# Seven-product turns with two weight buffers: another order of VectorE and ScalarE around cast and low part, the first down slab loaded in halves, the down unit begun on six tiles

## The reference, cut to what matters

```python
def swiglu(h, w_gate, w_up, w_down):
    return (jax.nn.silu(h @ w_gate) * (h @ w_up)) @ w_down
...
h = modulate(rms_norm(x, norm_ffn1[i]), sh1, sc1)
x = x + 0.5 * gt1[:, None, :] * swiglu(h, ffn1_gate[i], ffn1_up[i], ffn1_down[i])
...
h = modulate(rms_norm(x, norm_ffn2[i]), sh3, sc3)
x = x + 0.5 * gt3[:, None, :] * swiglu(h, ffn2_gate[i], ffn2_up[i], ffn2_down[i])
```

## Time and profile before

| | |
|---|---|
| median of 3 runs | 1463.26 us (1463.21 to 1464.64) |
| profiled execution, its own time | 1461.96 us |
| its span, first to last instruction | 1460.4 us |
| TensorE busy | 1380.3 us, 95% |
| VectorE busy | 1011.8 us, 69% |
| ScalarE busy | 571.6 us, 39% |
| mean granted clock of TensorE | 0.985 of full speed |

### The profile page before, as it was taken

The page is one execution under the profiler, slowest core; times in us unless marked ns, Lnnn a source line. Parts: engine busy times, 40 slices in busy tenths (PEclk is TensorE's granted clock), DMA queues, the critical chain, the costliest instruction groups (busy, mean ns, idle before and its releaser), DMA issues. The chain is left out here.

```text
span 1460.4 us, 28232 instructions
## 1 busy us (share of the span) xinstructions
PE 1380.3 (95%) x11590; PEld 1327.8 (91%) x11590; DVE 1011.8 (69%) x1619; ACT 571.6 (39%) x813; POOL 80.1 (5%) x120
## 2 busy tenths in 40 slices
PE   6999998999899999999999999999999999899986
PEld 5899997998898999999899997999899999899986
DVE  5447777358646588998998997855645877457745
ACT  5423454235435322534243337332532345225433
POOL 6100000000001000000000000000000000000000
PEclk9999999999999999999999999999999999999998
DMA  9754664462374222223334444526222231322221
GB/s 320 236 175 148 197 202 148 130 212 90 96 222 139 88 86 78 90 70 102 122 125 146 149 153 160 187 87 202 87 72 80 92 120 59 116 86 88 77 97 59
DMA packets 133210, 189.45 MB, mean 130 GB/s; under 512 B 5133, under 2 KB 113057, under 8 KB 132898
## 3 DMA queue, kind: packets, MB, share of 16 engines
q1 hardware_dynamic: 111900, 112.55, 24.5%
q0 software_dynamic: 17136, 66.87, 13.7%
q10 hardware_dynamic: 4070, 8.57, 1.6%
HBM read 173.73 MB, written 15.18 MB: 129 GB/s over the span
## 5 line engine op out<-in xcount | busy, mean ns | idle before, releaser
L1714 DVE TENSOR_TENSOR w_lo<-raw,w_hi 128x1024 fp32r<-128x1024 f32 x152 | 186.0, 1224 | 262.9 <-ACT w_hi L1244 262.9
L1244 ACT CAST w_hi<-raw 128x1024 fp32r<-128x1024 f32 x152 | 158.9, 1046 | 409.7 <-PE pu L652 380.3
L652 PE MATMUL pu<-h_hi,w_hi 128*128 128x260 f32 x1408 | 287.7, 285 | 4.6 <-DVE work L2443 2.8
L652 PE MATMUL pu<-h_hi,w_lo 128*128 128x260 f32 x1408 | 283.5, 283 | 0.0
L652 PE MATMUL pu<-h_lo,w_hi 128*128 128x260 f32 x1408 | 282.8, 282 | 0.0
L652 PEld LDWEIGHTS pu<-h_hi,w_hi 128*128 128x128 f32 x1408 | 216.9, 188 | 8.7 <-DVE w_lo L1714 4.9
L652 PEld LDWEIGHTS pu<-h_hi,w_lo 128*128 128x128 f32 x1408 | 216.8, 188 | 0.0
L652 PEld LDWEIGHTS pu<-h_lo,w_hi 128*128 128x128 f32 x1408 | 216.6, 188 | 0.0
L652 PE MATMUL pu<-f_hi,w_hi 128*128 128x260 f32 x704 | 146.3, 290 | 22.7 <-DVE f_lo L2020 22.7
L2168 DVE SCALAR_TENSOR_TENSOR d<-u,cw,d 128x512 f32<-128x512 f32 x240 | 163.1, 745 | 0.1
L652 PE MATMUL pu<-f_hi,w_lo 128*128 128x260 f32 x704 | 144.2, 287 | 0.0
(11 more groups left out here) (356 smaller groups left out, 2564.7 us busy)
## 6 DMA issues: line engine op xcount, KB each, us to landing
raw_a<-in_w_ada POOLq DMA_DIRECT2D x30, 1024.0 KB, 7.8
raw<-in_w_in SPq DMA_DIRECT2D x28, 1024.0 KB, 5.2
raw<-in_ffn_gate SPq DMA_DIRECT2D x32, 512.0 KB, 4.0
raw<-in_ffn_up SPq DMA_DIRECT2D x32, 512.0 KB, 5.0
raw<-in_ffn_down SPq DMA_DIRECT2D x16, 1024.0 KB, 5.4
gates_d<-sg_lb ACTq DMA_DIRECT2D x24, 260.0 KB, 2.5
raw<-in_ffn_up SPq DMA_DIRECT2D x6, 1024.0 KB, 5.4
raw<-in_ffn_down SPq DMA_DIRECT2D x8, 768.0 KB, 4.3
```

The costliest lines, as they stand in the source:

```text
L652: last = mm(pu[p][:, e, 0:HALF], w[p][:, k, :], m[:, k, e * HALF:(e + 1) * HALF], start=(at_k == 0 and j == 0), stop=(at_k == k_tiles - 1 ...
L1244: nc.scalar.copy(w_hi[p][:], raw[:, slot, :, p * P:(p + 1) * P]).then_inc(s_hi, 1)
L1714: V.tensor_tensor(w_lo[p][:], raw[:, slot, :, p * P:(p + 1) * P], w_hi[p][:].bitcast(F32), ALU.subtract).then_inc(s_lo, 1)
```

## The change

Seven edits in one:

1. On ScalarE the cast of hidden row 0 (L1372) moves from P1's place to P2's, behind the cast of the next block; the copies of adaLN rows go behind it. In the last turn Silu of row 0 goes ahead of the cast of the second down block.
2. On VectorE L2077 moves from behind the low part at P3 to ahead of it; L2066 from behind the low part at P2 to ahead of that at P5; L2049 from ahead of the low part at P4 to behind it; the low part of hidden row 1 (L2020) from P7's place to P2's, ahead of the low part, and that of row 0 behind it.
3. The weight sums of P3 and of P5 move from ahead of a low part to behind it, at the same position.
4. The sum of P3 uses the slot of that of P5 (`SUM_OF`), with a wait for the block that was there before (`BEFORE_IN_SLOT`).
5. In the last turn L2020 of row 1 and L2026 go ahead of the low part of the second down block.
6. SyncE loads the first down slab in two halves: the upper four row tiles when the last turn's sum of P6 is formed, the lower four when its P4 block is split. The first turn's loads go slot by slot.
7. The first down unit behind the turns begins when six of its tiles are there.

```diff
-SUM_OF = {P5: 0, P6: 1, P7: 2, P3: 3}
+SUM_OF = {P5: 0, P6: 1, P7: 2, P3: 0}
+BEFORE_IN_SLOT = {P5: P3, P6: P6, P7: P7}
@@ SyncE, loads
+                        if it == 0:
+                            for slot, w in enumerate((wg, wu)):
                                 sp.wait_ge(s_lo, n0 - 2 + 2 * slot)
+                                half_of(it, 0, s_raw0, slot, w)
+                                half_of(it, 1, s_raw1, slot, w)
+                            continue
+                        sp.wait_ge(s_wsum, 4 * (t - 1) + SUM_COUNT[P6])
                         rows_of(it, 0, s_raw0)
+                        sp.wait_ge(s_blo, TURN * (t - 1) + P4 + 1)
                         rows_of(it, 1, s_raw1)
+                    sp.wait_ge(s_wsum, 4 * t + SUM_COUNT[P6])
+                    sp.dma_start(raw[:, 0, 0:4, :], cols(wd, 0, 4, r0)).then_inc(s_raw0, 16)
                     sp.wait_ge(s_blo, TURN * t + P4 + 1)
-                    load(Lin(n0), 0, cols(wd, 0, r0=r0))
+                    sp.dma_start(raw[:, 0, 4:KT, :], cols(wd, 0, 4, r0 + 4 * P)).then_inc(s_raw[0], 16)
                     load(Lin(n0 + 2), 1, cols(wd, 256, r0=r0))
@@ TensorE, down unit
-                                 ready=(s_a, a0, GROUPS[g] - 1) if c == 0 else None, swap=g > 0 and c == 0)
+                                 ready=(s_a, a0, GROUPS[g] - (2 if g else 1)) if c == 0 else None, swap=g > 0 and c == 0)
@@ ScalarE, gate_turns
+                def silu_row0(t):
+
+                    act.wait_ge(s_c12, t + 1)
+                    af(gate[:, 0, :], gate[:, 0, :], ACT.Silu).then_inc(s_sg, 1)
...
-                        else:
-                            k = pos - P4
-                            split_hi(Lin(at[f"down{which}_{g}"] + k), k, 0)
+                        elif pos == P4:
+                            split_hi(Lin(at[f"down{which}_{g}"]), 0, 0)
                         if pos == P1:
                             nc.scalar.copy(halves(sg[:, 0, :]), psum(0)).then_inc(s_p1, 1)
-                            if it:
-                                hidden_hi(t - 1, it - 1, 0, 3)
-                        if pos == P2:
-                            ada_part(0, ADA_UP[g] + 2 * it, None)
+                        if pos == P2 and it:
+                            hidden_hi(t - 1, it - 1, 0, 3)
...
                             hidden_hi(t, it, 1, 2)
-                            act.wait_ge(s_c12, t + 1)
-                            af(gate[:, 0, :], gate[:, 0, :], ACT.Silu).then_inc(s_sg, 1)
+                            silu_row0(t)
                             if last:
+                                split_hi(Lin(at[f"down{which}_{g}"] + 1), 1, 0)
                                 hidden_hi(t, it, 0, 3)
+                        if pos == P2:
+                            ada_part(0, ADA_UP[g] + 2 * it, None)
@@ VectorE, add_weights
+                j = TURN * t + P5 if pos == P3 else TURN * (t - 1) + BEFORE_IN_SLOT[pos]
...
-                if t:
-                    dve.wait_ge(s_blo, TURN * (t - 1) + pos + 1)
+                if j >= 0:
+                    dve.wait_ge(s_blo, j + 1)
@@ VectorE, gate_turns: ahead of the low part
+                        if pos == P3 and last:
+                            right_half_row0(t)
+                            hidden_lo(t, it, 1, 2 * it + 1)
+                            multiplied_row0(t)
+                        if pos == P3 and not last:
+                            right_half_row0(t)
                         if pos == P2 and it:
-                            hidden_lo(t - 1, it - 1, 0, 2 * it)
+                            hidden_lo(t - 1, it - 1, 1, 2 * it - 1)
                         if pos == P5:
-                            add_weights(t, P3)
-                        if pos == P7:
-                            if it:
-                                hidden_lo(t - 1, it - 1, 1, 2 * it)
-                            dve.wait_ge(s_u3, 2 * t + 2)
+                            dve.wait_ge(s_p1, t + 1)
                             if it:
                                 dve.wait_ge(s_a, HIDDEN0 + a1 + 2 * it)
+                            V.tensor_tensor(gate_up[:, :, 2, 0:HALF], halves(sg[:, 0, :]), pair_b, ALU.add
+                                            ).then_inc(s_c11, 1)
+                        if pos == P7:
+                            dve.wait_ge(s_u3, 2 * t + 2)
...
-                        if pos == P4:
-                            dve.wait_ge(s_c22, t + 1)
-                            dve.wait_ge(s_sg, 3 * t + 1)
-                            V.tensor_tensor(gate[:, 1, 0:HALF], gate[:, 1, 0:HALF], pu[0][:, 1, 0:HALF], ALU.mult
-                                            ).then_inc(s_um, 1)
-                        if pos == P3 and not last:
-                            add_weights(t + 1, P5)
@@ VectorE, gate_turns: behind the low part
                         if pos == P1 and it:
                             multiplied_row0(t - 1)
-                        if pos == P2:
-                            dve.wait_ge(s_p1, t + 1)
-                            if it:
-                                dve.wait_ge(s_a, HIDDEN0 + a1 + 2 * it - 1)
-                            V.tensor_tensor(gate_up[:, :, 2, 0:HALF], halves(sg[:, 0, :]), pair_b, ALU.add
-                                            ).then_inc(s_c11, 1)
+                        if pos == P2 and it:
+                            hidden_lo(t - 1, it - 1, 0, 2 * it)
+                        if pos == P5:
+                            add_weights(t, P3)
                         if pos == P6 and not last:
                             add_weights(t + 1, P7)
                         if pos == P4:
+                            dve.wait_ge(s_c22, t + 1)
+                            dve.wait_ge(s_sg, 3 * t + 1)
+                            V.tensor_tensor(gate[:, 1, 0:HALF], gate[:, 1, 0:HALF], pu[0][:, 1, 0:HALF], ALU.mult
+                                            ).then_inc(s_um, 1)
                             dve.wait_ge(s_sg, 3 * t + 2)
...
-                        if pos == P3:
-                            dve.wait_ge(s_u2, 2 * t + 2)
-                            V.tensor_tensor(gate_up[:, :, 2, HALF:N], halves(sg[:, 1, :]), pair_c, ALU.add
-                                            ).then_inc(s_c12, 1)
-                            if last:
-                                hidden_lo(t, it, 1, 2 * it + 1)
-                                dve.wait_ge(s_c12, t + 1)
-                                multiplied_row0(t)
-                                hidden_lo(t, it, 0, 2 * it + 2)
+                        if pos == P3 and last:
+                            hidden_lo(t, it, 0, 2 * it + 2)
+                        if pos == P3 and not last:
+                            add_weights(t + 1, P5)
```

More of the change, by code:

```diff
@@ L267, in w_blocks, with raw0_loads, split_waits @@
             return t[j % 2][:].rearrange("p (s k) n -> p s k n", s=2)
+        def raw0_loads(t):
+            return 32 * (t + 1) + 16 * (t // TURNS)
+        def split_waits(eng, n):
+            for which in (1, 2):
+                for g in (1, 2):
+                    if n.i is None and n.base == at[f"down{which}_{g}"]:
+                        eng.wait_ge(s_raw0, raw0_loads(TURNS * (2 * which + g - 2) - 1) + 16)
         def raw_blocks(m2, k2):
@@ L431, in rows_of, with half_of @@
                         for slot, w in enumerate((wg, wu)):
-                            if it == 0 and k2 == 0:
-                                sp.wait_ge(s_lo, n0 - 2 + 2 * slot)
-                            c = r0 + 256 * it
-                            sp.dma_start(raw[:, slot, 4 * k2:4 * k2 + 4, :], cols(w, c, 4, 4 * k2 * P)).then_inc(sem, 16)
-                    for it, t in turns(which, g):
-                        if it:
-                            sp.wait_ge(s_wsum, 4 * (t - 1) + SUM_COUNT[P6])
+                            half_of(it, k2, sem, slot, w)
+                    def half_of(it, k2, sem, slot, w):
+                        c = r0 + 256 * it
+                        sp.dma_start(raw[:, slot, 4 * k2:4 * k2 + 4, :], cols(w, c, 4, 4 * k2 * P)).then_inc(sem, 16)
+                    for it, t in turns(which, g):
+                        if it == 0:
+                            for slot, w in enumerate((wg, wu)):
+                                sp.wait_ge(s_lo, n0 - 2 + 2 * slot)
+                                half_of(it, 0, s_raw0, slot, w)
+                                half_of(it, 1, s_raw1, slot, w)
+                            continue
+                        sp.wait_ge(s_wsum, 4 * (t - 1) + SUM_COUNT[P6])
                         rows_of(it, 0, s_raw0)
-                        if it:
-                            sp.wait_ge(s_blo, TURN * (t - 1) + P4 + 1)
+                        sp.wait_ge(s_blo, TURN * (t - 1) + P4 + 1)
                         rows_of(it, 1, s_raw1)
+                    sp.wait_ge(s_wsum, 4 * t + SUM_COUNT[P6])
```

(21 more changed lines are left out.)

2 lines of the change are left out of this document (removed).

## The result

The changed kernel takes 1427.35 us (median of four runs, 1425.86 to 1428.83), the kernel before beside it 1463.95 (1463.21 to 1464.99): a ratio of 0.975, 95% interval 0.973 to 0.977. The forecast was 1422, its range 1413 to 1440: right in sign, mechanism and range, 5 us short in size. In the profiled executions 1461.96 became 1428.83, and the span shrank by 33.2.

The account below looks back on a forecast made before the run. TensorE, at work in 95% of the span, was taken as the bound. Turns 15.7, down idle 18.7 and clock 6.7 sum to 41.1 us: 1461.96 to 1420.9, predicted as 1422 against the median of 1463.26; range 1413 to 1440.

Parts of the forecast that it names:

- P6 and P3: Waits inside a turn: 0.7 us at P6 goes with L1372 behind the cast, 0.9 at P3 with L2020 moved away.
- P5: Wait inside a turn: two sums of 1.22 us meet, about 0.35 late against 0.5 before; bounded from 0 to 1.5.
- P1, P4: Small waits inside a turn: a new 0.23 us at P1 behind L2049, and 0.1 at P4 as before.
- the turns: The four stages of seven-product turns, less idle at their ends: 359.4 us before, 343.7 after, so 15.7 won.
- Idle before the down units: TensorE's idle before the four first down units: 22.7 us falls to 4.0, so 18.7 won.
- Six tiles: First down unit: rows 1 and 0 just arrive in time; asking for seven tiles would start it 1.6 us later.
- Clock: First down units: with 0.7 to 1.5 us idle before them, 2.4 GHz throughout, 6.7 us won.
- the upper bound: Landing of the first down slab's lower half: 4.0 us taken, 5.1, the whole slab's time, as upper bound.
- Only the down units gain: Rival: the two sums at P5 cost 1.5 us, so the turns give nothing: 1438 us; chance 0.1.
- The half lands like the whole: Rival: the half slab lands 1.1 us later per stage, some clock loss stays: 1427 to 1436 us; chance 0.1.
- the slower rival: Lower rows land late at turn changes, up to 11.2 us, costing 5.1 more per turn: 1473 at ten; chance 0.03.

Follow-up runs that it names:

- the down edits alone: The kernel before with only the first down slab in halves, six tiles asked for and the change's first-turn loads: 1441.2 us, ratio 0.984.
- the sum for P5 first: The changed kernel with P5's weight sum ahead of the right half of row 0, and Silu of row 0 behind P5's cast: 1421.5 us, ratio 0.970.
- ScalarE's order back: The changed kernel with the cast of hidden row 0 again ahead of the next weights' cast at P1: 1431.35 us, ratio 0.978.

## Why the prediction was right, and by how much not

Trace against trace, 41.1 us were forecast and 33.1 came: 8.0 short (turns 4.3, clock 1.4, the rest of the kernel 2.2). That the medians are only 5 us off the forecast is luck in part: the profiled execution before lay 1.3 below its median, the one after 1.5 above.

- **P6 and P3: right.** Both waits went, and each comes back when its one order is undone.
- **P5: right to 0.05.** The chain was put at 2.41, 3.55, 4.65, 5.97, 6.11 behind P3's end. With that end at 1321.13 (ScalarE's cast of P2 begins 0.04 behind it, at 1321.17) the rows above give 2.42, 3.55, 4.69, 6.01 and 6.15. With the sum and the Silu moved the wait is gone. What the forecast did not see is that the wait need not stay.
- **P1, P4: right in sum.** 0.23 and 0.1 were expected; P3-P1 has 0.12, P1-P2 0.09, P7-P4 0.06. P4-P3 has 0.1, which I had at nothing. Middle turns took 20.98 instead of 20.8.
- **The term that was mis-sized: the turns, 15.7 against 11.4.** By stage, less idle: 92.9, 86.2, 85.0 and 84.0 against 90.5, 86.2, 83.7 and 83.3. Stage 1 has 2.4 of the 4.3: I reckoned that its adaLN slabs give the turns time, took the earlier trace rows only as a danger to the lower rows, and did not ask who waits for the upper ones. VectorE does, at the sum for P7, which stayed where it was, with P3's low part behind it (by the starts 1.25 in the first turn, 0.23 and 0.36 in two others); moving L2020 away took one of two causes of that wait; the same turns without that wait took 22.85, 0.2 over my 22.6. In stage 3 (1.3) the first turn and the last have 0.7 at P5 instead of 0.55 and 0.35; what is left there and the 0.7 of stage 4 are the 0.2 that each turn takes longer.
- **Idle before the down units: right in sum, and that by luck**: 18.7 against 18.7, but by stage 0.5, 2.2, 0.9, 0.4 against 0.7, 1.5, 0.9, 0.9. Both edits carry it: each undone costs some 9 or 10 us. The half slab took 3.55 to 3.8 in three stages and 5.07 in the fourth, the upper bound that I had set for another reason.
- **Six tiles: right.** No wait for L2048 is left at a down unit, and seven put 11.3 us of them back. I had 6.4 for the four; it is 7.3 of idle, and 10 with the clock.
- **Clock: 5.3 of 6.7.** Three down units ran at 1.00 behind idles of 0.4 to 0.9; the one behind 2.19 did not. The forecast took the wait of 2.0 for the old L2443 as a sign that such an idle leaves the clock alone; in the trace after, the same wait of 2.0 has a fall right behind it, at 923.0. Turns full of short waits ran at 1.00 throughout. That is against the rule of the Trainium skill's page that I weighed (TensorE: Matmul & The Clock Gate, "A second HAM failure mode: psum-queue depth-cycling"), as far as these turns go.
- **The rivals.** "Only the down units gain" would have been the 1441 of the down edits alone: out. "The half lands like the whole" held in one stage of four. Rows landed in up to 11.4 us, as the slower rival wanted, but the upper ones, at some 1.8 us in stage 1.
- **Outside the sum: 2.2 us.** The untouched stretch 437.0 to 1147.0 took 709.96 against 708.40, with that clock fall at 923.0, which the trace of before lacks; the 0.8 at the start is open.
- **Not tried alone:** L2066, L2049, the slot that P3's sum shares, and the first turn's loads. What each of them is worth is argued, not shown.

## What to carry to other kernels

When an order is changed on an engine that just fits, ask of every instruction that stays ahead of the bottleneck's next block not only when its inputs are computed but when they land, and put one that may wait for a load behind what the bottleneck needs next. A wait read as "two engines are full" can be a question of which of two goes first: here 0.4 us a turn went by swapping a 1.22 us sum with a 0.69 us one and letting the Silu behind it wait for one more cast. Undo each part alone before believing a sum; here parts of 15.6 and 23.0 stood against 36.6 and, measured again, 38.6.

## What the hardware showed beside

**A fetch of instructions delays a load.** The long fetches of one trace mostly lie 100 to 150 matmuls and as many weight loads apart, and at the same matmul in kernel after kernel (of the ten that met a half, nine began at matmul 3206 or 3207, one at 3212). With 32 matmuls more at the start it began at 3209, counted with these, and so 3.8 us earlier in the stage, ahead of the half slab. So it is TensorE's instruction stream that is fetched, and the late load hangs on where a block of it ends. The Trainium skill (Runtime: NRT & Kernel Launch, "Instruction fetch mechanics") has blocks of 16 KiB, 256 instructions. The trace agrees: packets of 16 KB, mostly some 125 matmuls with as many weight loads apart. The Trainium skill calls the cost of crossing a block mostly hidden; here one cost 1.8 us of idle, by way of the load that it held up.

**The same idle, two clocks.** An idle of 1.8 us before P3 in stage 1's first turn was followed by a fall to 1.2 GHz in the kernel with the sum for P5 first, and by none in the one with ScalarE's order back (windows of 10 us; the 0.83 is the granted clock):

```profile
175.00:185.00 10.00, 8.18 (x57) 7.82 (x59) 7.78 (x16) 3.31 (x6) 0.00 (x0) 0.83 0.19 63
```
```profile
175.00:185.00 10.00, 8.19 (x85) 7.08 (x83) 8.75 (x16) 4.67 (x7) 0.00 (x0) 1.00 0.15 52
```

The first of the two kernels also idled 3.30 us before stage 2's down unit, and no fall followed there, while the 2.19 us of the changed kernel had one:

```profile
390.99 0.36 PE L672 MATMUL pu<-f_hi,w_hi 128*128 128x260 f32 x1 [3.30 <-DVE sg_lb L2110]
...
387.69:396.80 9.11, 5.81 (x49) 5.84 (x49) 5.67 (x8) 5.58 (x8) 2.85 (x4) 1.00 0.78 259
```

So the length of one idle does not tell whether the clock falls behind it; what does is open. In the untouched stretch, too, a fall came at 859 to 925 us in most traces, and in some not.
